# Moving small loads, one store and the token transposes at the start of a two-block kernel

## What is computed

```python
# first block, for each of two layers
shift, scale, gate = split(silu(c) @ mod_w + mod_b)          # for c and for c_ctx
h = rms_norm(x, pre_g) * (1 + scale) + shift
p = split_projection(h @ w_in)
y = concat(rwkv_mixer(p[0:8]), short_conv_mixer(p[8:12]), diff_attention_mixer(p[12:16])) @ w_out
x = x + gate * rms_norm(y, post_g)
# second block
x = x + rmsnorm(attention_mixer(h, w_in, rel_bias, w_out), g); x = x + rmsnorm(swiglu(...), g)
x = x + rmsnorm(recurrent_mixer(h, ...), g);                   x = x + rmsnorm(swiglu(...), g)
```

## Time and profile before

| | us |
|---|---|
| median of three runs (lowest, highest) | 2886.73 (2880.16, 2898.10) |
| the profiled execution, its own time | 2880.16 |
| its span | 2878.4 |
| TensorE busy in the span | 2477.2 (86%) |
| VectorE, ScalarE, POOL busy | 1490.4, 907.9, 208.0 |
| from the start to the first projection matmul | 56.4 |

### The profile page before, as it was taken

The page is one execution under the profiler, slowest core; times in us unless marked ns, Lnnn a source line. Parts: engine busy times, 40 slices in busy tenths (PEclk is TensorE's granted clock), DMA queues, the critical chain, the costliest instruction groups (busy, mean ns, idle before and its releaser), DMA issues. The chain is left out here.

```text
span 2878.4 us, 47954 instructions
## 1 busy us (share of the span) xinstructions
PE 2477.2 (86%) x19638; PEld 1946.6 (68%) x19638; DVE 1490.4 (52%) x2445; ACT 907.9 (32%) x1473; POOL 208.0 (7%) x348
## 2 busy tenths in 40 slices
PE   6998989488597998959868988789999797799997
PEld 4776767387485765838756666668878565588785
DVE  4355522567726554157775667355542565555523
ACT  3234432111134344221114555332222344322221
POOL 0000000454000000026400000000000000000000
PEclk9999998699798999959978999899999999899998
DMA  8611112200021211200003121223333222233332
GB/s 278 220 43 36 32 45 61 25 4 3 2 59 44 59 37 37 73 4 4 4 9 97 58 59 44 66 66 95 95 92 100 87 59 66 59 95 99 91 95 73
DMA packets 300975, 185.10 MB, mean 64 GB/s; under 512 B 5730, under 2 KB 284916, under 8 KB 300668
## 3 DMA queue, kind: packets, MB, share of 16 engines
q1 hardware_dynamic: 286364, 150.50, 17.9%
q10 hardware_dynamic: 12480, 25.17, 2.5%
q0 software_dynamic: 1952, 6.87, 1.3%
HBM read 177.79 MB, written 4.71 MB: 63 GB/s over the span
## 5 line engine op out<-in xcount | busy, mean ns | idle before, releaser
L245 DVE TENSOR_TENSOR wlo<-wraw,whi 128x1024 fp32r<-128x1024 f32 (+1 forms) x276 | 333.7, 1209 | 511.4 <-ACT whi L238 493.0
L305 PE MATMUL PW<-hhi,whi 128*128 128x512 f32 (+1 forms) x1152 | 434.1, 377 | 64.2 <-DVE hlo L957 39.2
L306 PE MATMUL PW<-hhi,wlo 128*128 128x512 f32 (+1 forms) x1152 | 433.1, 376 | 0.0
L307 PE MATMUL PW<-hlo,whi 128*128 128x512 f32 (+1 forms) x1152 | 432.1, 375 | 0.0
L238 ACT ACTIVATE whi<-wraw 128x1024 fp32r<-128x1024 f32 (+1 forms) x276 | 287.5, 1043 | 284.7 <-PE PW L307 254.0
L305 PEld LDWEIGHTS PW<-hhi,whi 128*128 128x128 f32 x1152 | 220.3, 191 | 107.3 <-issue 53.5
L360 PE MATMUL PW<-hhi,whi 128*128 128x512 f32 (+1 forms) x640 | 242.5, 379 | 16.0 <-DVE hlo L857 9.4
L306 PEld LDWEIGHTS PW<-hhi,wlo 128*128 128x128 f32 x1152 | 220.2, 191 | 38.5
L307 PEld LDWEIGHTS PW<-hlo,whi 128*128 128x128 f32 x1152 | 220.0, 191 | 38.8
L362 PE MATMUL PW<-hlo,whi 128*128 128x512 f32 (+1 forms) x640 | 225.9, 353 | 0.0
L361 PE MATMUL PW<-hhi,wlo 128*128 128x512 f32 (+1 forms) x640 | 225.8, 353 | 0.0
(11 more groups left out here) (415 smaller groups left out, 4430.7 us busy)
## 6 DMA issues: line engine op xcount, KB each, us to landing
wraw<-in_w_in SPq DMA_DIRECT2D x68, 512.0 KB, 3.9
mod_w<-in_mod_w ACTq DMA_DIRECT2D x12, 2048.0 KB, 8.8
wraw<-in_ffn_w_gate SPq DMA_DIRECT2D x44, 512.0 KB, 3.8
wraw<-in_ffn_w_up SPq DMA_DIRECT2D x44, 512.0 KB, 3.8
wraw<-in_ffn_w_down SPq DMA_DIRECT2D x32, 512.0 KB, 3.7
wraw<-in_attn_w_in SPq DMA_DIRECT2D x24, 512.0 KB, 3.7
wraw<-in_w_out SPq DMA_DIRECT2D x16, 512.0 KB, 3.7
wraw<-in_rg_w_in SPq DMA_DIRECT2D x16, 512.0 KB, 3.9
```

What stands on the lines that cost most here:

```text
L245: dve.tensor_tensor(wlo[:, slot, 0:kb, :], wraw[:, slot, 0:kb, :], whi[:, slot, 0:kb, :].bitcast(F32), ALU.subtract).then_inc(S("w_split"), 1)
L305: pe.matmul(acc, whi[:, u % 2, k, :], rhi[:, k0 + k, s0:s1], start=a, stop=False)
L306: pe.matmul(acc, wlo[:, u % 2, k, :], rhi[:, k0 + k, s0:s1], start=False, stop=False)
L307: last_mm = pe.matmul(acc, whi[:, u % 2, k, :], rlo[:, k0 + k, s0:s1], start=False, stop=b)
```

## The change

Five edits, all but one inside the first phase.

1. The 33 loads of `VR` and the two of `lamb` are issued by ScalarE, ahead of everything else it does, and no longer by SP. SP goes on to the weight stream right after the tokens.
2. `diag` holds one matrix a tile instead of two. Half r of a tile is now the plain transpose of all eight pieces (r even, by the identity in `const`, waiting only for the tile to land) or all eight pieces times `diag` (r odd). VectorE copies each half with one instruction of 1024 elements a partition instead of two of 512.
3. The first four loads of `mod_w` are issued after T == 2 instead of T == 3.
4. The copies of the identity into `diag` are gone.
5. The store of `rel_bias_reversed` is issued by POOL right behind the load of the constants, and no longer behind `wup`.

```diff
@@ -422,7 +422,7 @@
         modT = place("modT", [P, DEPTH, 24, 2], at=at_mix + K1)
-        diag = place("x_roots_diagonal", [P, 2, 2, P], at=at_mix + 2 * K1)
+        diag = place("x_roots_diagonal", [P, 2, P], at=at_mix + 2 * K1)
         mrow = place("mod_rows_sb", [P, 2, 512], at=at_mix + 12 * K1)
@@ -449,9 +449,9 @@
 
-        def sp_rows(sp):
+        def act_rows(act):
             def rows(i, at, ap, n):
-                sp.dma_start(VR[at:at + n, i, :], ap).then_inc(S("vec_rows"), 16)
+                act.dma_start(VR[at:at + n, i, :], ap).then_inc(S("vec_rows"), 16)
                 n_rows[0] += 16
@@ -478,7 +478,7 @@
             for l in range(DEPTH):
-                sp.dma_start(lamb[:, l, :], t["diff_lambda"][l].rearrange("a b -> (a b)").unsqueeze(0)
+                act.dma_start(lamb[:, l, :], t["diff_lambda"][l].rearrange("a b -> (a b)").unsqueeze(0)
                               .to_broadcast([P, 256])).then_inc(S("lam_rows"), 16)
@@ -491,7 +491,6 @@
                 sp.dma_start(xtok[:, T, :], src).then_inc(S(f"x_landed{T}"), 16)
-            sp_rows(sp)
 
@@ -527,13 +526,16 @@
             for r in range(2 * NT):
-                T, b0 = r // 2, 4 * (r % 2)
+                T, rooted_x = r // 2, r % 2
                 if r >= 2:
                     pe.wait_ge(S("xT_ready"), r - 1)
-                pe.wait_ge(S("diag_made"), T + 1)
-                for b in range(4):
-                    ins = pe.matmul(PW[r % 2][:, b * 2 * P:(b + 1) * 2 * P], xtok[:, T, (b0 + b) * P:(b0 + b + 1) * P],
-                                    diag[:, T % 2, :, :], start=True, stop=True)
+                pe.wait_ge(*((S("diag_made"), T + 1) if rooted_x else (S(f"x_landed{T}"), 16)))
+                for b in range(NB):
+                    acc, src = PW[r % 2][:, b * P:(b + 1) * P], xtok[:, T, b * P:(b + 1) * P]
+                    if rooted_x:
+                        ins = pe.matmul(acc, src, diag[:, T % 2, :], start=True, stop=True)
+                    else:
+                        ins = pe.transpose(acc, src, ident)
                 ins.then_inc(S("xT_turned"), 1)
@@ -593,17 +595,15 @@
                 dve.wait_ge(S("xT_turned"), r + 1)
-                T, b0 = r // 2, 4 * (r % 2)
-                src = PW[r % 2][:, :].rearrange("p (b c n) -> p b c n", b=4, c=2)
-                dve.tensor_copy(xT[:, b0:b0 + 4, T * P:(T + 1) * P], src[:, :, 0, :])
-                dve.tensor_copy(xr[:, T, b0:b0 + 4, :], src[:, :, 1, :]).then_inc(S("xT_ready"), 1)
+                T = r // 2
+                src = PW[r % 2][:, :].rearrange("p (b n) -> p b n", b=NB)
+                dst = xr[:, T, :, :] if r % 2 else xT[:, :, T * P:(T + 1) * P]
+                dve.tensor_copy(dst, src).then_inc(S("xT_ready"), 1)
             for T in range(NT):
...
                     dve.wait_ge(S("xT_turned"), 2 * T - 2)
-                if T < 2:
-                    dve.tensor_copy(diag[:, T, 0, :], ident)
-                dve.tensor_scalar(diag[:, T % 2, 1, :], ident, xroot[:, T:T + 1], None, ALU.mult) \
+                dve.tensor_scalar(diag[:, T % 2, :], ident, xroot[:, T:T + 1], None, ALU.mult) \
                    .then_inc(S("diag_made"), 1)
@@ -674,6 +674,7 @@
         def act_inputs(act):
+            act_rows(act)
             act.wait_ge(S("cs_zeroed"), 1)
@@ -687,7 +688,7 @@
                 act.activation(xroot[:, T:T + 1], xln[:, T:T + 1], ACT.Exp, scale=-0.5).then_inc(S("x_root"), 1)
-                if T == 3:
+                if T == 2:
                     for i in range(MFIRST):
@@ -723,6 +724,7 @@
             pool.dma_start(const[:, NEARLY:], t["const"][:, NEARLY:]).then_inc(S("const_rest"), 16)
+            pool.dma_start(revd, rev[:, 0:LR].unsqueeze(1).to_broadcast([8, P, LR])).then_inc(S("rev_stored"), 16)
 
@@ -1435,8 +1437,6 @@
                 pool.dma_start(wup[:, 1, :], t["rwkv_a_up"][l].rearrange("d a n -> (d a) n")).then_inc(s_wup.sem, 16)
-                if l == 0:
-                    pool.dma_start(revd, rev[:, 0:LR].unsqueeze(1).to_broadcast([8, P, LR])).then_inc(S("rev_stored"), 16)
 
```

## The result

The changed kernel takes 2908.79 us (median of 6 runs, 2903.36 to 2913.43) against 2883.67 us of before on the same chip (6 runs): 25.1 us slower, ratio 1.008 with a 95% interval of 1.0053 to 1.0106. The forecast was 2930.

A forecast was written before the change was run, and what follows sets the result against it. TensorE, busy 2477.2 of 2878.4 us, was taken as the bound, so only its waits matter. Start 1.5 + stand 42 + cold clock 2 = 45.5 us over 2880.16 gave 2925.7, by the median 2932, forecast 2930; 8-in-10 range 2886 to 2945.

The forecast's parts named there:

- How two queues share an engine: DMA engines take one packet of each queue in turn, whatever its size, so short packets slow to the pace of long ones.
- the one on conv0: In conv0, load 5 of mod_w waits behind store packets, landing at about 122.5 us; TensorE, asking at 80.44, stands 42 us.
- The stand: TensorE waiting in conv0 for load 5 of mod_w, from 80.4 to 122.5 us: 42 us, bounded below by nothing.
- 64 x (0.79 + 0.09) = 56 us, and 2 us more: Load 5's delay: 64 packets each wait for a store packet on eight slow engines; 2 us for weight packets beside them.
- The start: First phase up to the projection, with small loads on ScalarE and changed transposes: moves by -4 to +4 us, taken as +1.5.
- the repeated 13.36: At the start, the first four mod_w issues hold ScalarE for 13.36 us again, as in the kernel before.
- the two sums: End of the last token copy: 32.5 + 3 x 3.8 = 43.9 or 36.2 + 11.4 = 47.6 us, against 44.11 before.
- The cold clock: TensorE's clock and pipe are cold after waiting for load 5 in conv0: 2 us lost, between 0 and 4.
- rival 1: In conv0 the store slips in beside the loads, which keep their times; only the start counts, about 2885 us; chance 0.20.
- rival 2: In conv0 load 5 needs half the rounds, so TensorE stands 15 us; total 2899, up to 2905 us; chance 0.11.
- rival 3: Projection begins 4 us sooner through a faster start, with the store hidden; total 2876 to 2883 us; chance 0.05.

## Why the prediction was wrong, step by step

**Direction and mechanism: right.** The step "How two queues share an engine" and the one on conv0 hold: load 5 is the victim, TensorE stands for it before rows 5, units 2 to 7 follow at 11.3 us, and nothing regains it in this phase. The store alone (26.2 us) is the whole loss.

**The step that failed: "in `rwkv prep` the store's leaving gives nothing, 0 us, as no one waited for it or beside it".** 9.5 us came back there. POOL itself waited for it, at its first drain. The number was in the earlier trace rows (484.10 + 54.3 = 538.4), but the prediction did not set it beside POOL's rows of the next phase, where an idle time of 8.91 us ends at 538.7 with no releaser. The twofold store (55.7 us of wait) and the store by ScalarE behind `wup` (0.41 us, with the same traffic still running) show that the wait is for POOL's own DMA. That it is the drain rests on the program's order: the other thing that stands between L1597 and L1600, the wait for ScalarE's exponentials, was met 8.6 us before POOL went on. A kernel without the drain was not tried.

**The stand: 42 forecast, 34.0 measured.** The term "64 x (0.79 + 0.09) = 56 us, and 2 us more" is mis-sized. It adds the loads' own packets to the store's. But the store keeps its pace of 50 GB/s beside them (of 1.48 MB in 20 us of the stand 0.99 are the store's), and its packet takes 0.44 x 16 x 20 / 193 = 0.73 us instead of 0.79. That fits a bound in the source partitions, which all eight engines share: while one engine serves a short packet, the others read faster. A turn of all three queues takes 8 x 20 / 193 = 0.83 us, where the store alone sent a packet an engine every 8 x 30 / 295 = 0.81 us. So 64 turns are 52 to 53 us and not 58, and load 5 landed at 116.0 instead of 122.5. That is 6.5 of the 8 us. The remaining 1.5 us are that TensorE asked at 82.0 instead of 80.4.

**The start: +1.5 forecast, +0.3 us at the first projection matmul, +1.5 at rows 4.** The parts were off in both directions. The four mod_w issues took 9.87 us instead of the repeated 13.36, and started at 22.2 instead of 21.0; the last token copy ended at 44.46 + 1.23 = 45.7, between the 43.9 and 47.6 of the two sums (44.1 before). That the total came out as said is luck in part. The start's edits alone give +0.1%.

**The cold clock: 2 forecast, 2.3 measured**: 3.64 - 1.92 = 1.7 in rows 5 and 0.6 in the unit behind.

**Sum.** Forecast 1.5 + 42 + 2 + 0 = 45.5. Measured 1.5 + 34.0 + 2.3 - 9.5 = 28.3, against the 28.6 us that ScalarE is late behind `rwkv prep` in the profiled execution, and 25.1 by the medians (15.3 to 30.6 by the interval). The forecast was also laid on a median of before of 2886.73, 3.1 us above the 2883.67 of six runs, and rounded down from 2932 to 2930. So rival 1 (slips in) is refuted by the stand, rival 2 (half the rounds) by 193 to 193, and rival 3, which was to gain at the start, by +0.1%. I had put 0.64 on a loss above 1%. It stayed below because both terms missed the same way: with the 9.5 us not regained it would have been 34.6 us, with the stand at 42 us 33.1, and either is above 1%.

## What to carry to other kernels

Before a slow DMA is moved, divide its busy share by its packets: this store, at 0.79 us a packet on eight engines, held every load beside it to one packet an engine in some 0.8 us, however short these are, and the load with the least slack paid. Look also for who waits where it leaves: an idle time with no releaser on the engine that issued a DMA, ending as that DMA lands, is suspect of being a wait for it, and a run with the DMA issued twice tells. Here it went when another engine issued the DMA, behind the loads that are needed. And a DMA that reads few partitions should have them spread: eight rows in partitions 0, 4 to 28 instead of 0 to 7 made a packet of this store nearly four times as fast, and beat the kernel before by 0.3 to 0.4% wherever the store stood.

## What had not been expected of the hardware

- POOL waits, at its first drain by the program's order, for the DMAs that it has issued: 8.9 us with one store under way, 55.7 with two, 0.4 with the same store still running in ScalarE's queue.
- Two stores issued by POOL in a row ran on different halves of the engines (48.8% busy with one, 97.6% with two), with 50 and 54 GB/s in all.
- The pace of the store was set by the partitions read: 0.79 us a packet from partitions 0 to 7, 0.21 us from every fourth.
